# Two matmuls of 256 columns for one of 512 in the looped feed-forward input projections

## The reference

```python
def swiglu(x, w_in, w_out):
    a, b = jnp.split(x @ w_in, 2, axis=-1)
    return (jax.nn.silu(a) * b) @ w_out
...
        h = h + FFN_RES * swiglu(rmsnorm(h, g_ff1[i]), w_ff1_in[i], w_ff1_out[i])
```

## Time and profile before

| what | value |
|---|---|
| median of 3 runs | 3403.47 us (3403.36 to 3406.96) |
| span of the profiled execution | 3401.4 us |
| between the span and the median | 2.1 us |
| TensorE busy | 3301.1 us, 97% of the span, 16322 matmul records |
| VectorE, ScalarE, GpSimd busy | 54%, 33%, 41% |

### The profile page before, as it was taken

One profiled execution on the slowest core, in us unless ns is written; L12 is line 12 of the kernel. 1 busy time (PEld: TensorE's weight loads), 2 busy tenths in 40 slices (PEclk: granted clock), 3 DMA queues, 4 the chain that ended last, 5 costly groups with the idle time before them and its releaser, 6 DMA issues.

```text
span 3401.4 us, 44063 instructions
## 1 busy us (share of the span) xinstructions
PE 3301.1 (97%) x16322; PEld 2611.0 (77%) x16322; DVE 1848.6 (54%) x2928; ACT 1113.3 (33%) x1836; POOL 1385.9 (41%) x691
## 2 busy tenths in 40 slices
PE   9999999999999999999999999999999999999998
PEld 7888877778888788887777888887776666777676
DVE  5532378875433464234888643335545648575753
ACT  4222234422222422223443222223234642344332
POOL 4444454444444344444544444443242223322342
PEclk9999999999999999999999999999999989999999
DMA  5333332244433334333313443344642222322221
GB/s 147 93 116 92 106 88 66 60 122 135 131 89 110 102 120 146 88 102 95 81 44 101 127 133 91 94 155 124 212 131 60 59 57 68 60 46 69 84 86 50
DMA packets 632956, 335.01 MB, mean 98 GB/s; under 512 B 97774, under 2 KB 622703, under 8 KB 631247
## 3 DMA queue, kind: packets, MB, share of 16 engines
q1 hardware_dynamic: 608062, 286.80, 30.4%
q10 hardware_dynamic: 23680, 44.32, 3.6%
q0 software_dynamic: 1040, 1.57, 0.1%
HBM read 308.65 MB, written 23.98 MB: 98 GB/s over the span
## 4 chain that ended last, share of the span: by engine, by line
PE 83%; DVE 11%; issue 3%; ACT 2%; POOL 0%; DVEq 0%; DMA 0%; ACTq 0%; POOLq 0%
PE ps L345 25%; PE ps L334 25%; PE ps L346 24%; PE ps L1138 2%; PE ps L1172 1%; PE ps L1162 1%; DVE UH L440 1%; PE ps L520 1%; DVE TURN L449 1%; DVE UL L443 1%; DVE ps L864 1%; DVE UL L855 0%; DVE SS L452 0%; DVE PRE L385 0%; PE ps L1289 0%
## 5 line engine op out<-in xcount | busy, mean ns | idle before, releaser
L270 POOL TENSOR_TENSOR WL<-RAW,WH 128x1024 fp32r<-128x1024 f32 (+4 forms) x606 | 1297.3, 2142 | 1977.3 <-ACT WH L292 1976.7
L345 PE MATMUL ps<-UH,WH 128*128 128x512 f32 x3056 | 1218.5, 399 | 48.1 <-DVE UL L855 16.4
L346 PE MATMUL ps<-UL,WH 128*128 128x512 f32 x3056 | 1195.8, 391 | 0.0
L292 ACT ACTIVATE WH<-RAW 128x1024 fp32r<-128x1024 f32 (+4 forms) x605 | 571.0, 945 | 1170.6 <-PE ps L334 1126.7
L334 PE MATMUL ps<-UH,WL 128*128 128x512 f32 x3056 | 802.7, 394 | 0.7 <-POOL WL L270 0.7
L345 PEld LDWEIGHTS ps<-UH,WH 128*128 128x128 f32 x3056 | 574.5, 188 | 206.5 <-issue 43.9
L334 PEld LDWEIGHTS ps<-UH,WL 128*128 128x128 f32 x3056 | 570.0, 187 | 132.9 <-issue 12.5
L346 PEld LDWEIGHTS ps<-UL,WH 128*128 128x128 f32 x3056 | 574.8, 188 | 121.4 <-issue 4.5
L345 PE MATMUL ps<-HH,WH 128*128 128x512 f32 x704 | 273.9, 389 | 0.0
L346 PE MATMUL ps<-HL,WH 128*128 128x512 f32 x704 | 273.9, 389 | 0.0
L385 DVE TENSOR_TENSOR PRE<-ps,R 128x512 f32<-128x512 f32 x144 | 99.4, 691 | 293.1 <-PE ps L334 289.4
(11 more groups left out here) (447 smaller groups left out, 3441.1 us busy)
## 6 DMA issues: line engine op xcount, KB each, us to landing
RAW<-w_ff_in SPq DMA_DIRECT2D x176, 512.0 KB, 3.8
RAW<-w_in SPq DMA_DIRECT2D x72, 512.0 KB, 3.9
RAW<-w_ff_out SPq DMA_DIRECT2D x64, 384.0 KB, 3.4
RAW<-w_ff_out SPq DMA_DIRECT2D x64, 320.0 KB, 3.1
RAW<-d_w_in SPq DMA_DIRECT2D x24, 512.0 KB, 3.8
CM<-cm_dram ACTq DMA_DIRECT2D x8, 1088.0 KB, 10.5
RAW<-b_w_in SPq DMA_DIRECT2D x17, 512.0 KB, 3.7
RAW<-w_out SPq DMA_DIRECT2D x16, 512.0 KB, 3.8
```

Source lines behind the costliest of these rows:

```text
L270: e.tensor_tensor(m.WL[:, s, 0:k, :], m.RAW[:, r, 0:k, :], m.WH[:, s, 0:k, :].bitcast(F32), ALU.subtract).then_inc(m.low_ready.sem, 1)
L292: e.activation(m.WH[:, s, 0:k, :], m.RAW[:, r, 0:k, :], ACT.Copy).then_inc(m.high_ready.sem, 1)
L345: e.matmul(out, m.WH[:, s, c, 0:t.cols], H[:, k0 + c, :], start=(x == 0 and c == 0), stop=False)
L346: e.matmul(out, m.WH[:, s, c, 0:t.cols], L[:, k0 + c, :], start=False, stop=False)
```

## The change

The class `Gemm` gets an attribute `parts`, the slices of the token axis that each matmul is cut into. For every `Gemm` it is one slice of 512; a new subclass `ByHalves`, used for the loop alone, has two slices of 256. Each matmul of 512 columns becomes two of 256, which write the left and the right half of the same bank.

```diff
+    parts = (slice(0, SEQ),)
...
-                        return e.matmul(out, m.WL[:, s, c, 0:t.cols], H[:, k0 + c, :], start=False, stop=last)
+                        for q, part in enumerate(self.parts):
+                            mm = e.matmul(out[:, part], m.WL[:, s, c, 0:t.cols], H[:, k0 + c, part], start=False, stop=last,
+                                          skip_group_check=len(self.parts) > 1)
+                        return mm
...
-                        e.matmul(out, m.WH[:, s, c, 0:t.cols], H[:, k0 + c, :], start=(x == 0 and c == 0), stop=False)
-                        e.matmul(out, m.WH[:, s, c, 0:t.cols], L[:, k0 + c, :], start=False, stop=False)
+                        for q, part in enumerate(self.parts):
+                            for half in (H, L):
+                                e.matmul(out[:, part], m.WH[:, s, c, 0:t.cols], half[:, k0 + c, part],
+                                         start=(x == 0 and c == 0 and q == 0 and half is H), stop=False, skip_group_check=len(self.parts) > 1)
...
+class ByHalves(Gemm):
+    parts = (slice(0, SEQ // 2), slice(SEQ // 2, SEQ))
...
-            add(Gemm(m, (FC - HELD) // 2, pair_of_tiles(HELD // 2), vec_per_iter=4, rhs_ready=u_ready, splits=2))
+            add(ByHalves(m, (FC - HELD) // 2, pair_of_tiles(HELD // 2), vec_per_iter=4, rhs_ready=u_ready, splits=2))
```

## The result

The changed kernel takes 3419.4 us (median of 3 runs, 3418.07 to 3420.05) against 3403.47 us: the ratio is 1.0042, with a 95% interval of 1.0028 to 1.0055. It is 15.9 us slower, where 15.4 us were forecast.

What follows compares the result with a forecast made beforehand. The prediction took TensorE, without idle time in the loops, to bound them: 3401.4 us (span) + 2.1 (around it) + 15.4 (1152 more matmul starts) = 3418.9 us, loads and issue adding nothing. The range was 3402 to 3436 us.

Steps and rivals of the forecast that it cites:

- There is no idle time in these loops to fill: In the four loops TensorE is always busy, so the change costs what it does to the distance between matmul starts.
- Others, waits, issue: Around the loops' matmuls: other engines, unchanged waits and doubled instruction issue cost nothing; about -0.2 us at loop heads left out.
- 1152 more matmul starts, +15.4 us: In the four loops each instruction carries a fixed 0.0133 us, so a half takes 0.1200 us: +15.4 us.
- the excess: In the loops, the 0.0133 us per matmul by which 0.2267 us exceeds 512 columns at one a cycle, 0.2133.
- 1152 more weight loads, nothing: In the four loops each half's load can follow every 0.11 us, below 0.1200, so it is hidden: no cost.
- the column rival: In the loops the 0.0133 us belongs to the columns: no change, 3403.5 to 3405.8 us; chance 0.30.
- the load rival: In the loops weight loads become the bound: a half at 0.124 us adds 24.5 us, 3428.0 us; chance 0.18.

## Why the forecast came true, and where its reasoning did not

- **What bounds.** "There is no idle time in these loops to fill": so it was, and it is what made the number computable. The growth is 1152 times the growth of a pair, 0.2400 against 0.2267 us.
- **Others, waits, issue.** "No cost" for the others and for issue held: windows and counts of the other engines are unchanged, and loads were not shared (17474). At the head of the second loop the second wait is 0.31 instead of 0.37 us. From its first matmul to the first one behind it, the first and the fourth loop grew by 3.83 us, the second and third by 3.71 and 3.68: 0.27 us less in all, about the 0.2 that the forecast named and left out.
- **1152 more matmul starts, +15.4 us.** This step failed. "If each instruction carries 0.0133 us" was taken as the value. With loads short enough (64 weight columns, or bf16 with elements 4 bytes apart) a pair of halves costs what a whole does, so there a start costs 0 to 1.8 ns, and nearly all of the excess goes with the columns. (With 8 weight columns it is 4.4 ns a start.) My two arguments for a fixed step (a round amount, none of it at the lower clock) fit a cost by column just as well, and I had said so in the rival.
- **1152 more weight loads, nothing.** This step failed too, by the same amount the other way. "It is hidden, with 0.01 us to spare" compared 0.11 with 0.12 us. But the alternatives were 0.1116 us for the loads alone and 0.1133 us for the matmuls alone, and together they take not the greater of the two but 0.1200. All of the 13.3 ns a pair, 2 x 6.7, is there with full loads, gone with 64 weight columns and, but for some 2 ns, with the bf16 load of 97 ns.
- So the forecast of 3418.9 us was right by two errors that cancel. The right case was a mixture of two rivals: the column rival's matmul, with a milder form of the load rival's collision, at 0.1200 instead of 0.124. That 0.124 was no pace of loads, and this too is a slip in the reading of the earlier trace rows. The transposes in the kernel before:

```profile
775.36 1.03 PE L2441 MATMUL ps<-IDENT,PB 128*128 128x128 f32 x8
```

Their first load starts at 775.13 and their second with the first transpose, at 775.36: the first of the eight distances is 0.23 us, and the other seven, 0.76 us up to 776.12, are 0.11 each.

What the load does to the matmul is not settled. The load itself takes 192 ns among halves and 188 among whole matmuls, so it is not left alone either; whether the matmul slows it or the load just ahead does is not shown. The Trainium skill ("TensorE: Matmul & The Clock Gate", Step-by-step: what each phase is for) says that loading the next tile's weights does not steal read bandwidth from the running matmul, having a port of its own. For whole matmuls the trace agrees: 0.2267 us with loads of 8 columns and of 128. For halves the runs show a cost of the load all the same, 0.1133 us with a load of 134 ns and 0.1200 with one of 192, but not that it is bandwidth. Whether the two reads meet, or the exchange of weights does, no run here tells. Nor is it known why 8 weight columns cost 2.2 ns more than 64.

## What to carry to other kernels

Where matmuls follow each other without a gap, the price of cutting them is the change of the distance between starts times their number, and it can be read from a few rows. Two activities that each just fit under the bound may together exceed it, as 0.1116 us of load and 0.1133 us of matmul made 0.1200: don't book the shorter one as free. And a forecast that comes out to the microsecond still needs its terms tested one by one; the first row of the changed loop already hinted against mine.

## What the runs showed of the hardware

- At full clock, with loads short enough, a matmul whose moving elements lie 4 bytes apart takes about 6% over a column a cycle, bf16 or fp32r (0.1133 us for 256 columns, whose cycles are 0.1067; 0.2267 and 0.2250 for 512). In the one run with elements 2 bytes apart, and a constant operand, it took 2.5 ns over its columns (0.1092 us for 256).
- Full fp32r loads of 128 columns follow each other every 0.1116 us beside matmuls of 128 columns. Beside matmuls of 256 columns, which take 0.1133 us with a load of 134 ns, they make it 0.1200.
- Where fp32r and bf16 matmuls alternate, the load of the bf16 matmul starts only with its matmul, while that of the fp32r one starts with the matmul ahead of it. A pair takes 0.463 us, more than two fp32r matmuls (0.453).
